# Tails of the two expert stages: stores of the last expert from two engines, key/value weights held back, the combine by diagonal products in layer 1, a square root in place of log and exp

## The reference, cut to what matters

```python
def layer_norm(x, g, b):
    mu = jnp.mean(xf, axis=-1, keepdims=True)
    var = jnp.mean(jnp.square(xf - mu), axis=-1, keepdims=True)
    return ((xf - mu) * lax.rsqrt(var + LN_EPS) * g + b)
...
    for e in range(MOE_EXPERTS):                 # 16 experts, each row uses 2 of them
        h = jax.nn.silu(xt @ w_gate[e]) * (xt @ w_up[e])
        y = y + comb[:, e:e + 1] * (h @ w_down[e])
...
        m = hier_moe(x, ...)
        x = layer_norm(ALPHA * x + m, p['ln_g'][layer, 1], p['ln_b'][layer, 1])
        if layer == DEPTH_A - 1:
            kv_new = jnp.einsum('btd,dgsnh->btgsnh', x, p['b_w_kv'])
```

## Time and profile before

| what | value |
|---|---|
| runs | 1718.04, 1713.45, 1716.48 us; median 1716.48 |
| the profiled execution | 1710.88 us, its span 1709.1 us |
| PE, DVE, ACT, POOL busy | 92%, 34%, 21%, 11% of the span |
| weight loads (PEld) busy | 68% |
| mean granted TensorE clock | 0.968 of full |
| layer 0's experts end (last copy out of PSUM) | 854.1 us |
| layer 0's combine, norm and key/value products | 854 to 980 us |
| layer 1's experts end | 1650.9 us |
| layer 1's spill pass, combine and norm | 1651 to 1709 us |

### The profile page before, as it was taken

How to read it: one execution, slowest core, us unless ns; L and a number is a source line. 1 busy time by engine, 2 the same in 40 slices (tenths; PEclk the granted TensorE clock), 3 DMA queues, 4 the chain that set the end, 5 groups by cost and what they waited for, 6 DMA issues and landing times. The chain is left out here.

```text
span 1709.1 us, 46599 instructions
## 1 busy us (share of the span) xinstructions
PE 1572.6 (92%) x20620; PEld 1160.8 (68%) x20620; DVE 584.1 (34%) x1561; ACT 364.6 (21%) x911; POOL 196.4 (11%) x190
## 2 busy tenths in 40 slices
PE   7999999997899899999959999999999989999980
PEld 6878868885668455555548788887878755555550
DVE  5121445665464421212154010005755522121215
ACT  1123334432501011111132001104650101111113
POOL 1000014643400300000020000000000020000002
PEclk9999999999889999999989999999999999999995
DMA  9500001000550999999981186661125389999984
GB/s 287 180 33 25 1 2 36 29 29 29 183 210 25 332 369 377 385 377 379 374 249 64 43 154 130 126 117 63 65 79 208 138 272 381 377 385 377 387 319 156
DMA packets 218262, 331.32 MB, mean 194 GB/s; under 512 B 70504, under 2 KB 117408, under 8 KB 218064
## 3 DMA queue, kind: packets, MB, share of 16 engines
q1 hardware_dynamic: 193648, 285.33, 49.0%
q0 software_dynamic: 8208, 25.57, 5.6%
q10 hardware_dynamic: 16208, 17.44, 2.9%
HBM read 295.94 MB, written 32.39 MB: 192 GB/s over the span
## 5 line engine op out<-in xcount | busy, mean ns | idle before, releaser
L2062 PE MATMUL bank<-ring_extra,xT 128*32 128x256 f32 x3600 | 201.0, 382 | 0.9 <-DVE xT L1740 0.9
L2529 PE MATMUL bank<-x_early,ring 128*128 128x256 f32 (+1 forms) x768 | 171.1, 383 | 3.2 <-DMA ring<-in_b_w_q 1.7
L2062 PEld LDWEIGHTS bank<-ring_extra,xT 128*32 128x32 f32 x3600 | 115.2, 110 | 79.4 <-issue 4.3
L2529 PEld LDWEIGHTS bank<-x_early,ring 128*128 128x128 f32 x768 | 144.9, 190 | 26.1 <-issue 2.6
L2062 PE MATMUL bank<-ring,xT 128*32 128x256 f32 x2544 | 141.3, 380 | 0.9 <-DVE xT L1740 0.9
L1745 DVE TENSOR_TENSOR sg<-sg,bank 128x128 f32<-128x128 f32 x96 | 27.0, 281 | 295.9 <-ACT sg L1927 295.9
L2062 PEld LDWEIGHTS bank<-ring,xT 128*32 128x32 f32 x2544 | 81.4, 110 | 55.4 <-issue 2.0
L1927 ACT ACTIVATE sg<-bank 128x128 f32<-128x128 f32 x96 | 26.6, 277 | 351.3 <-PE bank L2062 351.3
L386 PE MATMUL bank<-mix,ring 128*128 128x260 f32 x448 | 100.5, 384 | 0.0
L2080 PE MATMUL bank<-ring_extra,hT 128*32 128x256 f32 x1680 | 96.6, 380 | 0.4 <-issue 0.4
L386 PEld LDWEIGHTS bank<-mix,ring 128*128 128x128 f32 x448 | 84.5, 190 | 15.3 <-ACT k L568 2.4
(11 more groups left out here) (428 smaller groups left out, 2320.6 us busy)
## 6 DMA issues: line engine op xcount, KB each, us to landing
ring_extra<-in_moe_w_gate SPq DMA_DIRECT2D x75, 512.0 KB, 10.4
ring_extra<-in_moe_w_up SPq DMA_DIRECT2D x75, 512.0 KB, 12.7
ring_extra<-in_moe_w_down SPq DMA_DIRECT2D x37, 1024.0 KB, 14.9
ring<-in_moe_w_down SPq DMA_DIRECT2D x29, 1024.0 KB, 15.0
ring<-in_moe_w_gate SPq DMA_DIRECT2D x57, 512.0 KB, 10.3
ring<-in_moe_w_up SPq DMA_DIRECT2D x57, 512.0 KB, 13.0
ring<-in_a_w_rkv SPq DMA_DIRECT2D x12, 1024.0 KB, 10.3
expert_out<-yo ACTq DMA_DIRECT2D x128, 96.0 KB, 6.4
```

The costliest lines, as they stand in the source:

```text
L2062: ins = pe.matmul(ps[u][32 * q:32 * q + 32, 0:256], xT[:, kt, 32 * u:32 * u + 32], gate_up(w, kt % 2, q), start=kt == 0, stop=kt == KT - 1)
L2529: ins = pe.matmul(ps[2 * (job % 3) + h][:, 0:n], w[:, kt_, rr, :], z[:, kt_, lo:lo + n], start=kt_ == 0, stop=kt_ == 7)
```

## The change

1. The last expert's four stores are split: ACT issues r = 0 and 1, and SP r = 2 and 3 after it has waited for `yc` to reach 48. In both layers.
2. In layer 0 SP issues the first two chunks of the key/value weights as before and the other four after `ys` says that all experts' stores have landed.
3. ACT loads the norm's gain and shift before it copies the last expert's result, and no longer after the last stores.
4. In layer 1 the combine is moved to PE: DVE makes, per tile and choice, a 128x128 diagonal matrix of the weights (ten tensor_scalar instructions, into `xT` and `yo[0]`), and PE sums in two banks of PSUM the rows times the identity and the two gathered rows times their diagonals, six products of 512 columns per tile. The products with the identity run two tiles ahead. ACT's row sum then reads the two banks and writes the rows back. `centred` and `normalise` of DVE follow, with the buffer of the second gather between them.
5. In layer 0's norm ACT makes one Sqrt and DVE a reciprocal in place of Ln and Exp; a Sqrt of one column is put ahead of the norm in both layers.
6. The banks of PSUM are allocated in pairs.

```diff
-        self.banks = [stack.enter_context(nc.psum_tensor(f"bank{i}", [128, 512], F32)) for i in range(8)]
+        self.bank_pairs = [stack.enter_context(nc.psum_tensor(f"banks{i}", [128, 1024], F32)) for i in range(4)]
+        self.banks = [pair[:, 512 * h:512 * h + 512] for pair in self.bank_pairs for h in range(2)]
...
     def vector(dve):
...
         def normalise(i):
...
+            dve.wait_ge(root, i + 1)
+            dve.reciprocal(mv[0:n, t, 2:3], mv[0:n, t, 2:3]).then_inc(ag, 1)
+            dve.wait_ge(ag, 2 * i + 2 if kv else i + 1)
             dve.wait_ge(scaled, i + 1)
-            dve.scalar_tensor_tensor(rows[0:n, t, :], rows[0:n, t, :], mv[0:n, t, 2:3], shift[0:n, :], ALU.mult, ALU.add).then_inc(final, 1)
+            src = rows[0:n, t, :] if kv else pair[i][0:n, 1, :]
+            dve.scalar_tensor_tensor(rows[0:n, t, :], src, mv[0:n, t, 2:3], shift[0:n, :], ALU.mult, ALU.add).then_inc(final, 1)
+
+        def centred(i):
...
+            dve.wait_ge(combined, i + 1)
+            dve.wait_ge(totals, i + 1)
+            dve.wait_ge(centre, i + 1)
+            dve.scalar_tensor_tensor(pair[i][0:n, 1, :], rows[0:n, t, :], mv[0:n, t, 1:2], gain[0:n, :], ALU.add, ALU.mult).then_inc(scaled, 1)
...
         else:
-            statistics(0)
-            for i in range(1, TILES):
-                statistics(i)
-                normalise(i - 1)
+            dve.wait_ge(ys[0], 64 * (EXPERTS // 2))
+            for i in range(TILES):
+                t = order[i]
+                n = tile_rows(t)
+                for k in range(2):
+                    dve.tensor_scalar(spread(i, k)[0:n, 0:n], core.c("ident")[0:n, 0:n], plan["weights"][0:n, k, t:t + 1], None, ALU.mult).then_inc(spread_made, 1)
+            for i in range(TILES):
+                centred(i)
+                if i:
+                    normalise(i - 1)
             normalise(TILES - 1)
...
     def sync(sp):
...
-        feed.upto(sp, 6 * EXPERTS, next_stop, every)
+        feed.upto(sp, 6 * EXPERTS, next_stop - (4 if kv else 0), every)
+        sp.wait_ge(yc, SUBS * EXPERTS)
+        for r in (2, 3):
+            sp.dma_start(out_rows(EXPERTS - 1)[r], yo[(EXPERTS - 1) % 2][32 * r:32 * r + 32, :, :]).then_inc(ys[(EXPERTS - 1) % 2], 16)
+        if kv:
+            for b in range(2):
+                sp.wait_ge(ys[b], 64 * (EXPERTS // 2))
+            feed.upto(sp, 6 * EXPERTS, next_stop, every)
         sp.wait_ge(core.slot_free, core.held_by[v_slots[-1]] + 1)
         sp.wait_ge(d, steps["plan"])
         n = spills(sp)
...
     def scalar(act):
...
-            for r in range(4):
+            for r in range(4 if e + 1 < EXPERTS else 2):
...
+            else:
+                act.wait_ge(xt, 2 * EXPERTS)
+                act.dma_start(gain[:, :], io["ln_g"][layer, 1:2, :].to_broadcast([128, D])).then_inc(got, 16)
+                act.dma_start(shift[:, :], io["ln_b"][layer, 1:2, :].to_broadcast([128, D])).then_inc(got, 16)
             if e:
                 results(e - 1)
...
-            act.activation(spare, r, ACT.Copy, accum_out=mv[0:n, t, 0:1]).then_inc(totals, 1)
+            act.activation(r, combined_in(i)[0:n, :], ACT.Copy, accum_out=mv[0:n, t, 0:1]).then_inc(totals, 1)
...
-            act.activation(mv[0:n, t, 2:3], mv[0:n, t, 3:4], ACT.Ln).then_inc(root, 1)
-            act.activation(mv[0:n, t, 2:3], mv[0:n, t, 2:3], ACT.Exp, scale=-0.5).then_inc(root, 1)
+            act.activation(mv[0:n, t, 2:3], mv[0:n, t, 1:2], ACT.Sqrt, bias=eps[0:n, :]).then_inc(root, 1)
...
     def tensor(pe):
...
+        def add_residual(i):
+            pe.wait_ge(sums, t + 1)
+            if i >= 4:
+                pe.wait_ge(totals, i - 3)
+            for h in range(2):
+                pe.matmul(combined_in(i)[0:n, 512 * h:512 * h + 512], core.c("ident")[0:n, 0:n], rows[0:n, t, 512 * h:512 * h + 512], start=True, stop=False)
+
+        def add_pair(i):
+            pe.wait_ge(spread_made, 2 * i + 2)
+            for k in range(2):
+                pe.wait_ge(gat[i][k], 16)
+                for h in range(2):
+                    ins = pe.matmul(combined_in(i)[0:n, 512 * h:512 * h + 512], spread(i, k)[0:n, 0:n], pair[i][0:n, k, 512 * h:512 * h + 512], start=False, stop=k == 1)
+            ins.then_inc(combined, 1)
+
+        if not kv:
+            add_residual(0)
+            add_residual(1)
+            for i in range(TILES):
+                add_pair(i)
+                if i + 2 < TILES:
+                    add_residual(i + 2)
```

39 lines of the change are left out of this document (17 added, 22 removed).

## The result

| what | before | after |
|---|---|---|
| median of the runs | 1716.70 us (4 runs, 1713.45 to 1718.04) | 1745.03 us (4 runs, 1741.20 to 1749.52) |
| ratio | | 1.0166, 95% interval 1.0137 to 1.0195 |
| the profiled execution, its span | 1710.88, 1709.1 us | 1741.20, 1739.2 us |
| PE, DVE, ACT, POOL busy | 92%, 34%, 21%, 11% | 92%, 33%, 20%, 11% |

The change makes the kernel 28.3 us slower. 19.5 us were forecast, with a range that ends at 1743: the direction was right, the size was too small.

A forecast was written before the change was run, and what follows sets the result against it. PE, busy 92%, was taken as the bound, with the change touching only its two tails. Layer 0 +5.0, spill pass +11.5 and combine +3.0 make 19.5 us, on 1716.5 giving 1736.0 us, range 1727 to 1740, outer bounds 1722 and 1743.

The forecast's parts named there:

- Layer 0, stores and first gather: Layer 0's tail: stores all landed by 856.6, POOL's first gather at 856.9, 7.1 us earlier.
- Of these 0.9 us belong to the split: Layer 0's first gather: of 7.1 us gained, 0.9 come from splitting the stores, 6.2 from the hold.
- Layer 0, the held weights: Layer 0's tail: held chunks land behind the gathers, PE stops some 8 us, first product at 882.5; layer 0 +5.0 us.
- two rows of unmixed queues: Layer 0's transfers: chunks 12.7 us and gathers 13.0 us, one after the other 25.7 us, ending at 883.3.
- the row of mixed queues: Layer 0's transfers: rate with gather and weights mixed, 0.63 MB in 2 us, gives 27 us and 884.6, a bound.
- Clock loss: Layer 0's first key/value products: PE restarts at the half clock after its stall, 1.9 us lost.
- Rival 1: Layer 0: held weights land in time, tile 0 sets the start, -5.3 us; sum +9.2, 1725.7 us; chance 0.15.
- Layer 1, the spill pass: Layer 1's tail: list and gather issued behind SP's wait and stores, PE's turn at 1663.7 instead of 1652.16, +11.5 us.
- nothing is added: Layer 1's spill pass: PE restarts cold, but did so in part before, so no extra time.
- Layer 1, the combine: Layer 1's combine: the bound moves from DVE to PE, 5.3 us per tile, and does not fall; +3.0 us.
- PE has made its identity products by 1673 and idled 5 us.: Layer 1's combine: identity products done before the first gather at 1678.2, PE's clock then fallen, first four instructions 3.5 us.
- Sqrt: Layer 0's norm: Sqrt for Ln and Exp removes table loads worth 0.6 us, swallowed by the wait for weights.

The follow-up runs named there:

- x4: The changed kernel with nothing held, all six key/value chunks issued before SP's two stores, split kept: +28.2 us against before, ratio 1.0176.
- y3: The kernel before with the hold of four key/value chunks alone, ACT issuing all stores: +10.5 us against before, ratio 1.0056.
- x1: The changed kernel with SP's stores in layer 0 alone, ACT issuing all four in layer 1: +15.0 us against before, ratio 1.0098.
- x3: The changed kernel with layer 1's combine on DVE as before, early Sqrt kept: +22.2 us against before, ratio 1.0130.
- z1: The changed kernel with the loop over spill passes of 2 rounds instead of 15 in all engines: +23.4 us against before, ratio 1.0151.
- y1: The kernel before with only layer 0's Sqrt for Ln and Exp and the early Sqrt: +3.3 us against before, ratio 1.0012.

## Why the prediction fell short

1. **Layer 0, stores and first gather: nearly right.** Forecast 856.9 for POOL on the scale of before, 2.8 us after the last copy; it was 4.6. SP, which waits for the stores, went on 3.8 us after the first of them was issued, where 2.5 had been forecast (854.1 to 856.6). "Of these 0.9 us belong to the split" is not borne out: without the hold the gather came 2.8 us later (x4), and beside the hold 1.4 us earlier (y3 against after), both together with the earlier gain and shift.
2. **Layer 0, the held weights: mechanism right, size 2.4 us short.** PE did stop behind tile 0's turn for `in_b_w_kv`, at the half clock. The first product was forecast 28.4 us after the last copy and came at 31.3. Of the difference 1.3 us are the late stores, passed on to the weights, and 1.6 the bytes: from SP's issue to PE's start 27.5 us instead of 25.9. I took a value near the sum of two rows of unmixed queues; the row of mixed queues, 27 us and 1 of start, was the better one. What the sum took for granted, that the engines stay full to the last byte, did not hold: from 878 to 882 us their share was 1.06, from 882 to 886 it was 0.54, at 173 GB/s. Why, no run shows. x1, x3 and z1 keep this part of the change and have the first product at 29.5, 30.1 and 29.2, so the miss is 0.8 to 2.9 us. Clock loss: 1.9 forecast; the 384 key/value products take 86.7 us against 84.7 before, 2.0 us (87.4 to 87.7 in x1, x3 and z1). With the first product's 5.9 us that makes 7.9; the 7.4 measured over the whole stretch is as near as that stretch can tell. The sum took 882.6 where the text had chosen 882.5. Rival 1 fell.
3. **Layer 1, the spill pass: right, 1.9 us short.** The list's issue came 3.0 us after the last copy, as forecast. Its landing took 2.3 us instead of 1.9, the gather 8.0 instead of 7.0 (the 7.9 us of the earlier trace rows was the better row), and "nothing is added" for the cold restart missed 0.4 us on the turn (1.08 against 0.68). x1 removes this term and nothing else, and gives back 13.3 us of total.
4. **Layer 1, the combine: this step failed.** "PE has made its identity products by 1673 and idled 5 us." PE's program has the spill loop between its last product and the first one of the combine, and a loop over up to 15 passes of which one has work still steps through 14 empty rounds, at 0.74 us each (z1). The identity products came after the first gather had landed, at half clock, and the first pair was summed 11.2 us after the landing (taken as 4.5 us from its issue) instead of 5.3. These 5.9 us are the miss. The empty rounds make 4.7 of them, which z1 gives back. The other 1.2 are the first pair itself, for which 5.3 us were forecast and which takes 6.5 at half clock in z1. From there the forecast holds: 19.5 us from ACT's first to its last row sum (1710.91 to 1730.45), forecast 19.4; 5.15, 5.15 and 5.44 us from one full tile to the next, forecast 5.3. The order of PE's instructions showed where the products stand; what it takes to get there, past 14 empty rounds, no row of before priced, and I set it to nothing without saying so.
5. **Sqrt: right for the sum.** The 0.6 us is swallowed, and even without the hold PE's idle products hide the 0.5 us that DVE gains (y1).
6. **The sum.** 5.0 + 11.5 + 3.0 was forecast, 7.4 + 13.4 + 8.7 measured. The misses of 2.4, 1.9 and 5.7 all lie on one side: the choices between two bounds leaned to the row without load, and the last miss had no bound at all.

## What to carry to other kernels

Ahead of each wait that an edit puts into an in-order engine, list all that this engine issues behind it: here one wait for the last copy, put there for two stores, cost 13 us in the stage that nobody meant to touch. Where transfers are held back to clear the queues, release them when the urgent ones have landed, and let the consumer wait for each piece at its first use (31.3 to 22.5 us here); then look again at what was hidden, since PE's idle products, and the empty rounds ahead of them, had become the next bound (22.5 to 19.4). A loop with a fixed number of rounds is not free when it stands ahead of work on the critical path, even if all rounds but one are empty.
